# Feed-forward over the whole sequence in three slabs, spread normalisations and compact V tiles in a four-layer hybrid trunk on eight cores

## What is computed

```python
for l in range(4):                                  # x: (8, 2048, 1024)
    proj = x @ w_in[l]                              # xa, gb, gc, p, uv
    ya = gb * causal_conv3(gc * xa, w_conv[l])      # 384 wide
    yb = multiscale_pool(p) @ w_pool[l] * scale     # 256 wide, trailing means minus token
    u, v = split(gelu(uv))                          # 384 each; v normalised per head of 64
    yc = u * (tril(w_spatial[l]) @ v + b_spatial)   # per chunk of 128 tokens and head
    h = LN(ALPHA * x + concat(ya, yb, yc) @ w_o[l])
    g, up = split(h @ w_gate_up[l])                 # 2816 each
    x = LN(ALPHA * h + (silu(g) * up) @ w_down[l])
```

## Time and profile before

| | |
|---|---|
| median of 3 runs | 2726.2 us (2715.73 to 3064.77) |
| profiled execution | 2724.94 us, its span 2723.4 us (slowest core; the others from 2690.1) |
| granted TensorE clock, mean of each core | 0.977 to 0.987 |
| TensorE / VectorE / ScalarE / GpSimd busy | 96 / 45 / 30 / 18% |
| DMA | q0 (weights) 182.61 MB, 41.1% of 16 engines; q1 (x, transposes, small) 57.28 MB, 12.0% |

### The profile page before, as it was taken

The page is one execution under the profiler, slowest core; times in us unless marked ns, Lnnn a source line. Parts: engine busy times, 40 slices in busy tenths (PEclk is TensorE's granted clock), DMA queues, the critical chain, the costliest instruction groups (busy, mean ns, idle before and its releaser), DMA issues.

```text
span 2723.4 us, 36811 instructions; the slowest of 8 cores (2690.1 to 2723.4 us)
## 1 busy us (share of the span) xinstructions
PE 2602.2 (96%) x12320; PEld 1193.8 (44%) x12320; DVE 1222.1 (45%) x2257; ACT 814.1 (30%) x1465; POOL 478.6 (18%) x813
## 2 busy tenths in 40 slices
PE   6899999999799899999979989999998999999998
PEld 3444444444344344444434434444444444444443
DVE  4776325123666532522366752252236684225225
ACT  4643113102553311320255431131026533012111
POOL 3421011000441111110034110110004312001010
PEclk9999999999899999999989999999999999999999
DMA  7648463744534765384453474547437449356352
GB/s 164 123 84 96 82 101 64 115 67 73 96 65 86 87 89 94 61 121 71 69 97 67 85 93 81 101 68 111 82 58 109 75 70 130 53 97 146 52 101 74
DMA packets 183096, 242.25 MB, mean 89 GB/s; under 512 B 128512, under 2 KB 130688, under 8 KB 182912
## 3 DMA queue, kind: packets, MB, share of 16 engines
q0 software_dynamic: 53120, 182.61, 41.1%
q1 hardware_dynamic: 129792, 57.28, 12.0%
HBM read 384.68 MB, written 8.39 MB: 144 GB/s over the span
## 4 chain that ended last, share of the span: by engine, by line
PE 87%; DMA 6%; ACT 2%; issue 2%; DVE 1%; POOL 1%; SPq 0%; DVEq 0%; POOLq 0%; ACTq 0%
PE P L660 42%; PE P L688 22%; PE P L490 13%; PE P L639 8%; DMA XT<-XB 5%; PE P L505 2%; ACT VN L526 1%; DMA W<-w_chunks 1%; DMA W<-w_v 1%; PE P L539 0%; POOL SM L520 0%; DVE X L461 0%; PE P L608 0%; ACT XB L435 0%; PE P L447 0%
## 5 line engine op out<-in xcount | busy, mean ns | idle before, releaser
L660 PE MATMUL P<-XT,W 128*128 128x512 bf16 x5632 | 1236.2, 383 | 20.2 <-DVE BIG L665 20.2
L660 PEld LDWEIGHTS P<-XT,W 128*128 128x128 bf16 x5632 | 555.0, 99 | 698.8 <-issue 66.2
L665 DVE TENSOR_TENSOR BIG<-P,E 128x512 bf16<-128x512 f32 x352 | 242.9, 691 | 920.6 <-PE P L660 857.0
L688 PE MATMUL P<-W,BIG 128*128 128x512 bf16 x2816 | 610.4, 379 | 0.0
L664 ACT ACTIVATE E<-P 128x512 f32<-128x512 f32 x352 | 209.4, 596 | 1197.8 <-PE P L660 1197.7
L490 PE MATMUL P<-XT,W 128*128 128x512 bf16 x1792 | 419.3, 391 | 18.6 <-DVE X L461 11.7
L688 PEld LDWEIGHTS P<-W,BIG 128*128 128x128 bf16 x2816 | 275.6, 98 | 332.2
L472 DVE SCALAR_TENSOR_TENSOR X<-X,P 128x512 f32<-128x512 f32 x384 | 260.9, 685 | 311.4 <-PE P L688 283.1
L490 PEld LDWEIGHTS P<-XT,W 128*128 128x128 bf16 x1792 | 177.5, 100 | 234.9 <-issue 51.8
L390 POOL DMA_DIRECT2D W<-w_gu_t x176 | 103.9, 601 | 781.6 <-PE P L660 383.5
L459 ACT ACTIVATE XB<-X,MV 128x1024 bf16<-128x1024 f32 x128 | 146.8, 1147 | 280.0 <-DVE MV L457 266.8
(11 more groups left out here) (60 smaller groups left out, 967.9 us busy)
## 6 DMA issues: line engine op xcount, KB each, us to landing
W<-w_gu_t POOLq DMA_DIRECT2D x176, 512.0 KB, 10.8
W<-w_dn_t POOLq DMA_DIRECT2D x80, 512.0 KB, 5.2
W<-w_chunks POOLq DMA_DIRECT2D x56, 512.0 KB, 7.7
X<-x SPq DMA_DIRECT2D x16, 512.0 KB, 9.8
W<-w_o_t POOLq DMA_DIRECT2D x16, 512.0 KB, 5.3
out<-X SPq DMA_DIRECT2D x16, 512.0 KB, 2.6
W<-w_v POOLq DMA_DIRECT2D x16, 384.0 KB, 5.9
GBUF<-ln_g SPq DMA_DIRECT2D x8, 512.0 KB, 6.0
```

Source lines behind the costliest of these rows:

```text
L660: r = e.matmul(o.handle[:], lhsT=wv[:, h, k, :], rhs=XT[:, k, c:c + 512], start=(k == 0), stop=(k == 7))
L665: S.add("dve", lambda e: e.tensor_tensor(out=act_ap(ml, 4 * n, 4), in0=pu.handle[:], in1=t.handle[:], op=ALU.mult), reads=[pu, t], writes= ...
L688: r = e.matmul(pv.handle[:], lhsT=act_ap(kk, t, 1), rhs=wd[kk // 2].handle[:, o:o + 512], start=(kk == 0), stop=(kk == SLAB - 1))
```

## The change

1. The feed-forward goes over the whole sequence in three slabs of 6, 8 and 8 blocks (`SLABS`), so each weight is read once a layer. In slab 0 all six gate/up weights are held and the four groups of 512 tokens come one after the other, each over six blocks; in slabs 1 and 2 each weight is used for all four groups. The activations of a slab fill BIG as [block, token]. Each down stage covers 16 tiles with 3, 4 and 4 buffers of w_dn_t; the last one normalises.
2. `after1` normalises tiles 0 to 7 as before; tiles 8 to 15 are put on a list and taken off one per `gate_up` of the first two groups of slab 0 (`catch_up`), each tied to the product before it. MV grows from 6 to 12 buffers.
3. The square's discarded result goes to a buffer of its own, JUNK.
4. V is written without the zeros (384 columns in place of 768); each head's product goes to its own 64 partitions. The memsets of VN go. NVN is 10, the S pool has 6 buffers in place of 4. `conv` takes two T buffers in place of three.
5. For odd tiles the V normalisation is done on VectorE (subtract and multiply) in place of six ScalarE instructions.
6. The planner reckons a transpose at 1.3 us and 600,000 bytes, adds 1 us (`SAFE`) before a matmul that reads another engine's result, and has changed durations for square, power and norm. The loads of the second normalisation's factors and of the next layer's small weights move into slab 1.

```diff
+SAFE = 1.0
+                slack = SAFE if s.eng == "pe" and not op.dma and op.eng != "pe" and op.idx in s.raw else 0.0
+                s.ready = max(s.ready, op.end + slack + (LAT if self.needs_sem(s, op) else 0.0))
-SLAB = 11
-NVN = 8
+SLABS = ((0, 6), (6, 8), (14, 8))
+NVN = 10
+NORM_DVE = (1,)
-        VNB = [sb(f"VN{p}", [128, 768], BF16) for p in range(NVN)]
+        VNB = [sb(f"VN{p}", [128, SW], BF16) for p in range(NVN)]
+        S.pool("J", [sb("JUNK", [128, D], BF16)])
-        S.pool("S", [sb(f"S{p}", [128, SW]) for p in range(4)], {"L": 2})
+        S.pool("S", [sb(f"S{p}", [128, SW]) for p in range(6)], {"L": 2})
-                      dur=0.5, nbytes=262144)
+                      dur=1.3, nbytes=600000)
-        def layer_norm(i, mv):
-            xb = S.vt("XB")
+        def layer_norm(i, mv, cell=()):
+            xb = S.vt("J")
+                if i % 2 in NORM_DVE:
+                    S.add("dve", lambda e: e.tensor_scalar(out=r(2), in0=r(0), scalar1=1.0 / 64, scalar2=None, op0=ALU.mult), reads=[(sm, 0), sm], writes=[(sm, 2)], dur=0.16)
+                    S.add("dve", lambda e: e.tensor_tensor(out=v3(V.handle), in0=v3(V.handle), in1=r(2).unsqueeze(2).to_broadcast([128, 6, 64]), op=ALU.subtract),
+                          reads=[V, sm, (sm, 2)], writes=[V], dur=0.56)
+                    S.add("dve", lambda e: e.tensor_tensor(out=v3(vn.handle), in0=v3(V.handle), in1=r(6).unsqueeze(2).to_broadcast([128, 6, 64]), op=ALU.mult),
+                          reads=[V, sm, (sm, 6)], writes=[vn], dur=0.56)
+                    return vn
-                            r = e.matmul(m.handle[:, t * 128:(t + 1) * 128], lhsT=vns[t].handle[:, (2 * j + h) * 128:(2 * j + h + 1) * 128], rhs=WMT[:, 2 * j + h, :],
-                                         start=(h == 0), stop=(h == 1))
+                            r = e.matmul(m.handle[64 * h:64 * h + 64, t * 128:(t + 1) * 128], lhsT=vns[t].handle[:, (2 * j + h) * 64:(2 * j + h + 1) * 64], rhs=WMT[:, 2 * j + h, :],
+                                         start=True, stop=True)
-                ta, z, tb = S.vt("T"), S.vt("T"), S.vt("T")
+                ta, z = S.vt("T"), S.vt("T")
+                tb = ta
+        def ffn(l, after, catch_up, nxt):
+            for si, (m0, nm) in enumerate(SLABS):
+                if si == 0:
+                    ws = [wload(w_gu_d[l, m0 + ml]) for ml in range(nm)]
+                    for n in range(NG):
+                        for ml in range(nm):
+                            gate_up(ws[ml], ml, n)
+                            if n < 2 and n + ml > 0:
+                                catch_up([("BIG", ml - 1, 4 * n)] if ml else [("BIG", nm - 1, 0)])
+                else:
+                    for ml in range(nm):
+                        w = wload(w_gu_d[l, m0 + ml])
+                        for n in range(NG):
+                            gate_up(w, ml, n)
+                        if si == 1 and ml == 0:
+                            load_gb(l, 2)
+                        if si == 1 and ml == 0 and nxt is not None:
+                            load_small(nxt, [("BIG", 0, 0)])
+                wd = [wload(w_dn_d[l, (m0 + kk) // 2]) for kk in range(0, nm, 2)]
+                for i in range(NT):
...
+            def catch_up(cell):
+                if late:
+                    i, mv = late.pop(0)
+                    S.shift = 60
+                    layer_norm(i, mv, cell)
+                    cast_transpose(i)
+                    S.shift = 0
```

111 lines of the change are left out of this document (46 added, 65 removed).

## The result

| | before | after |
|---|---|---|
| median | 2725.7 us | 2633.9 us (2631.2 to 2680.2, 4 runs) |
| span of the slowest core; the others from | 2723.4; 2690.1 | 2634.7; 2627.0 |
| granted TensorE clock, mean of each core | 0.977 to 0.987 | 0.993 to 0.995 |
| q0, weights | 182.61 MB | 113.39 MB |

The ratio is 0.967, interval 0.963 to 0.971: 3.3% faster. The forecast was 2680 us with a range from 2640 to 2720. The direction was right, the time lies 46 us under the forecast and 6 us outside the range, and rival 2 (2652 us) came nearest.

The account below looks back on a forecast made before the run. It took TensorE, busy 96% of the span, as the bound, with 172.3 us of standing or slow running to win. 2724.9 - 32 + 8 - 13 - 5 - 9 + 5 = 2679, given as 2680 us from the median; range 2640 to 2720.

Parts of the forecast that it names:

- rival 2: Mixers: the remaining waits go as well, since the planner's new transpose cost gives a non-blocking order; 2652 us, chance 0.22.
- Feed-forward, booked -32: Feed-forward starts: few loads beside the late transposes remove the stalls, 6 of 38.2 us left; -32 us, bounds 0 and -38.
- Tail, booked +8: Layer 4's last slab: VectorE's normalisations take longer per tile than 3.45 us of matmuls; +8 us, bounds +4 and +14.
- Compact V, booked 0: Gating products with 64-column weights: 11 us saved if halves overlap, 22 lost if weight loads stand open; booked 0.
- Rival 4: Gating products: 64-column weights are slow, their loads standing in the open; 2702 us, chance 0.07.
- Mixers, booked -22: Mixers: two waits at the start, V norms and a denser VectorE, booked -13, -5, -9 and +5 us.
- -13 for the first wait: Mixers' start: weights loaded earlier remove the 5.9 us wait and its slow clock in layers 2 and 3; bounds -14.5 and 0.
- -5 for the second: Mixers' start: the 8.7 us wait behind ScalarE's transpose stall partly goes; -5 us, bounds -17 and +25.
- -9 for the V norms and buffers: Mixers: half of TensorE's 18.4 us wait for V norms goes, by the norm split, buffers and margin; bounds 0 and -25.
- +5 for a denser VectorE: Mixers: VectorE has about 108 us a layer and up to 9 for leftover tiles, in 125; +5 us, bounds 0 and +21.
- Rival 3: Mixers: late tiles' transposes meet chunk loads, so the second wait comes three times and VectorE costs +21; 2710 us, chance 0.17.
- Rival 5: Slab 0: late transposes take 7.2 us each beside loads and ScalarE holds the silus; slower than before, 2812 us, chance 0.05.

Follow-up runs that it names:

- e4: Kernel after, with a gate/up weight loaded anew for each group of 512 tokens in slab 0, 24 loads instead of 6; ratio 1.022 to the kernel before.
- e10: Kernel after, with each slab 0 gate/up load used for two token groups, 12 loads instead of 6; ratio 0.977 to the kernel before.
- e8: Kernel after, with tiles 8 to 15 normalised straight behind the residual instead of one per gate/up step; ratio 0.972 to the kernel before.
- e1: Kernel before with the new feed-forward alone; mixers, buffers, square into XB and planner's numbers stay old; ratio 0.978 to the kernel before.
- e14: Kernel after, with every V tile normalised on VectorE instead of odd tiles only; ratio 1.013 to the kernel before.
- e3: Kernel after, with the planner's old durations and no margin before TensorE; ratio 0.972 to the kernel before.
- e13: Kernel after, with every V tile normalised on ScalarE and the planner told its true duration; ratio 1.002 to the kernel before.
- e12: Kernel after, with the last normalisation's second pass of even tiles on ScalarE and GpSimd; ratio 0.969 to the kernel before.

## Why the prediction was right where it was, and where it failed

**Feed-forward, booked -32, measured -38.** The mechanism was right, and its rows came as named: no wait in steps n = 0 and 1, the late tiles' transposes 4.2 us apart (3.5 said), stages of 455.8 us (457 to 459 said). e4 shows the cause from the other side, e10 its edge. Four details were wrong. Spreading the late tiles counted for the argument, and e8 shows that it does nothing. The 6 us left over leaned on layer 4's 3.0 us, which is one stretch at the granted clock of 0.81 and no stall; about 12 of the 38 us are such stretches, and that none of them came after is not the mechanism's doing as far as any run shows. The "7.2 us each" was read from a line with a count: the transposes took 1.2 us of the queue, and the landing was what was slow. And all this was read from one core, while the feed-forwards' loss struck the cores unequally, 16.7 to 41.1 us; only the slowest core's share is won.

**Tail, booked +8, measured +8.1.** VectorE's first pass over the last tiles, from the timeline of after:

```profile
2613.99 1.28 DVE L465 SCALAR_TENSOR_TENSOR X<-X,MVB,GBUF 128x1024 f32<-128x1024 f32 x1
...
2617.78 1.28 DVE L465 SCALAR_TENSOR_TENSOR X<-X,MVB,GBUF 128x1024 f32<-128x1024 f32 x1
...
2621.57 1.28 DVE L465 SCALAR_TENSOR_TENSOR X<-X,MVB,GBUF 128x1024 f32<-128x1024 f32 x1
```

Its pitch per tile is 3.79 us, a little under the 3.9 that the sum took as its lower case. By the sum's own rule that gives 16 x (3.79 - 3.45) = 5.4 us, so the mechanism carries two thirds of the 8.1 us, and the exact agreement is luck.

**Start of layer 1, booked 0, measured 0.** By luck: the two cores read happen to agree. The row was booked as unchanged, but the mixers' edits act there too: the mean over the eight cores falls from 44.0 to 41.5 us.

**Compact V, booked 0.** Here the step that failed is "nearest is unchanged". The lower bound was the truth: two halves of 64 partitions run at once (in the trace after they start in pairs, some 3 ns apart, a pair per 56 ns), 24 products in 0.86 us for 1.50, about 10 us over the 16 groups of the span. Rival 4, slow 64-column weights, is dead: in no wait and in no row does a weight load of 64 columns hold up a product.

**Mixers, booked -22, measured -58.5.** This is the step that failed. The terms were -13 for the first wait, -5 for the second, -9 for the V norms and buffers, +5 for a denser VectorE, and their lower bounds -14.5, -17, -25 and 0. The lower bounds add up to -56.5, with compact V's 8 us in these layers to -64.5; the measured value lies between. The waits that were named did go (the first in the timeline, the V norms' from 18.4 to 2.1 us), so the places were right and their size was not: the choice inside the bounds failed, each time on the same side. The first two terms can be held against a run: with the slabs alone (e1) the mixers gain 33 us, where 18 were booked and 31.5 was the bound. All the other edits together bring 25 on top of that, where 9 less 5 were booked. The runs show two reasons.

First, the terms were weighed one by one, each at about half, as if the others stayed as they were. The runs say that they don't: the split brings 1 to 3 us on the old order and 50 or more on the new one; the planner's numbers bring 20.6 us here and cost on the kernel before. The mixers' edits act as one group. Read as one, the bounds of the group, 0 and near -57, would have been the thing to weigh, and not four halves of them; the runs take values all over that stretch and past both ends (losses of 17 to 107 us), so no run shows that the middle was impossible.

Second, the slow clock was booked at 1.4 us after each of two waits. The windows put 20 us of the 58.5 into busy time of the same matmuls: 7.7 of them can be the compact products, and some 12.6 are left to the clock, of which some 6 are the two stretches at 0.81 and some 7 the lower level, 1.2 GHz, behind waits (TensorE is busy for 29.6 us at that level before, for 9.9 after). The two granted levels cost 216 and 425 ns a matmul, so what stands beside each wait has to be counted with it.

The +5 for VectorE, "about 108 us a layer, dense", was neither right nor wrong by size: VectorE is at 151.5 of 187.5 us in the whole stage and TensorE still waits only 6.3. e14 shows where density becomes a cost: at 163 us the stage grows by 12.

**Rivals.** Rival 2 had the right direction and came nearest, but expected 28 us more where 46 came, and its source, the planner's view of the transposes, is only part of it: all the planner's numbers and the margin are worth 20.6 us (e3), 9 of them the margin, and the slabs gave the mixers 33 without them. Rival 3 did not come: even in e8 no crowd of late transposes holds anything up. Rival 5 was worked out with transposes of 7.2 us in slab 0; e4 made just that case and ended 2.2% above before, by the mechanism and near the size (+100 in the feed-forwards said, 141.8 measured; 2812 us said, 2770.8 to 2798.6 measured). What was slow was the landing, not 7.2 us of the queue for each. Its condition, loads during the late tiles, is what the slabs avoid.

**What stays open.** Why a V norm comes 7 us late in e13 with ScalarE at 107 of 211 us cannot be read from any one window; every variant gets another order from the planner, so that each number above is the price of an edit and of its new order together. Fixing the order and changing one duration would part the two, and was not tried. Open too is where the stretches at a granted clock of 0.81 come from: core 1 before has 91 us of them, after none, e14 158 us or more on every core.

## What to carry to other kernels

When several edits ease the same crowded stage, book them as one group with its own bounds, not as a sum of half-believed terms, and test by taking one out as well as by putting one in: the two answers differed here by about 50 us. Keep bulk weight loads out of the stretch in which DMA transposes feed TensorE; an order that asks for each weight once and early does that, whatever it saves in bytes. Where the slowest core sets the time, read a stall on all cores before pricing it, and look at the granted clock of each stage before calling a loss a wait. A line of the timeline with a count is a stretch, not one instruction's time.

## What the runs showed of the hardware

- Products with 64-column weights into different halves of the PSUM partitions overlap: 24 in 0.86 us, where 24 full-width ones took 1.50 us.
- A DMA transpose takes 1.23 us of the queue and 3.1 us to landing in the median (after); beside a load per 3.45 us the longest landing of a core is 29.6 to 39.5 us (e4), beside one per 6.9 us 9.7 to 30.2 us (e10).
- A VectorE pass of 128x1024 goes from 1.27 to 2.33 and 2.98 us while GpSimd adds 128x1024 (e12).
- Besides its two levels the granted clock shows stretches at 0.81 under dense matmuls: 15 us each before, 152 us on two cores of e8, where such a core ends some 27 us later.
